# Last tile's expert rows on GpSimd, and the first token copy between two groups of control words, in a two-layer diffusion trunk with routed experts

## The reference, cut to what matters

```python
x = post_norm(x, concat([ya, yb, yc]) @ w_out[l], g_a, ln_g[l, 0], ln_b[l, 0])
h = x * (1.0 + sc_f) + sh_f
x = post_norm(x, moe_ffn(h, ...), g_f, ln_g[l, 1], ln_b[l, 1])

# moe_ffn: top-1 of 4 groups, then top-2 of the 8 experts of that group
grp = argmax(softmax(x @ w_rg)); le = (x @ w_re) of that group
top_l, top_i = top_k(le, 2); top_w = softmax(top_l) * g_w
# the tokens are sorted by expert, each expert is a gated MLP:
out = (silu(xb @ w_g[e]) * (xb @ w_u[e])) @ w_d[e]
```

## Time and profile before

| | |
|---|---|
| median of 3 runs | 1551.4 us (1550.9 to 1553.43) |
| profiled execution, its own time | 1556.95 us |
| span of its instructions | 1555.1 us |
| mean granted clock of TensorE | 0.964 of full speed |
| PE busy | 1425.6 us (92%) |
| PEld busy | 1092.0 us (70%) |
| DVE busy | 612.9 us (39%) |
| ACT busy | 335.2 us (22%) |
| POOL busy | 366.3 us (24%) |
| HBM | 341.25 MB read, 32.07 MB written |

### The profile page before, as it was taken

How to read it: one execution, slowest core, us unless ns; L and a number is a source line. 1 busy time by engine, 2 the same in 40 slices (tenths; PEclk the granted TensorE clock), 3 DMA queues, 4 the chain that set the end, 5 groups by cost and what they waited for, 6 DMA issues and landing times.

```text
span 1555.1 us, 25254 instructions
## 1 busy us (share of the span) xinstructions
PE 1425.6 (92%) x9681; PEld 1092.0 (70%) x9681; DVE 612.9 (39%) x1453; ACT 335.2 (22%) x853; POOL 366.3 (24%) x471
## 2 busy tenths in 40 slices
PE   7999999898998999997899999999888989999964
PEld 5889899665887766563488889876577876556441
DVE  1121333578378322211452123348756852221116
ACT  2211211464111111110141121236430111111102
POOL 0100015542451312111010000754227321121101
PEclk9999999999998999998999999989899989999987
DMA  9410111674817999999642111157343499999974
GB/s 381 125 65 33 64 65 36 220 284 187 327 66 280 367 387 419 419 418 418 251 125 77 47 65 33 68 169 273 141 158 127 154 363 386 420 418 418 417 293 174
DMA packets 76741, 355.37 MB, mean 229 GB/s; under 512 B 20464, under 2 KB 23792, under 8 KB 43088
## 3 DMA queue, kind: packets, MB, share of 16 engines
q1 hardware_dynamic: 43056, 292.66, 47.8%
q0 software_dynamic: 20416, 46.73, 8.3%
q10 hardware_dynamic: 13152, 14.37, 2.9%
HBM read 341.25 MB, written 32.07 MB: 240 GB/s over the span
## 4 chain that ended last, share of the span: by engine, by line
PE 75%; DVE 8%; DMA 8%; issue 4%; POOL 3%; ACT 1%; SPq 1%; ACTq 0%; DVEq 0%; POOLq 0%
PE bank L1166 22%; PE bank L1531 15%; PE bank L1552 7%; DMA ring<-in_w_exp 4%; PE bank L1402 4%; PE bank L955 2%; PE bank L1150 2%; PE bank L858 2%; PE bank L1325 2%; DMA att<-mod_rows 2%; PE bank L1512 2%; PE bank L1299 1%; PE bank L1112 1%; PE bank L1115 1%; PE bank L881 1%
## 5 line engine op out<-in xcount | busy, mean ns | idle before, releaser
L1166 PE MATMUL bank<-ring,hT 128*128 128x256 f32 (+1 forms) x1600 | 340.9, 373 | 1.1 <-DVE z L2242 1.1
L1166 PEld LDWEIGHTS bank<-ring,hT 128*128 128x128 f32 x1600 | 293.5, 192 | 37.5 <-issue 1.6
L1531 PE MATMUL bank<-z,att 128*64 128x256 f32 (+2 forms) x960 | 181.0, 398 | 10.9 <-DMA ring<-in_w_exp 10.5
L1531 PEld LDWEIGHTS bank<-z,att 128*64 128x64 f32 (+2 forms) x960 | 118.8, 152 | 49.4 <-DMA ring<-in_w_exp 11.4
L1402 PE MATMUL bank<-ring,hT 128*128 128x256 f32 x640 | 142.7, 382 | 1.7 <-ACT hT L1838 1.1
L1402 PEld LDWEIGHTS bank<-ring,hT 128*128 128x128 f32 x640 | 121.2, 192 | 17.5 <-issue 2.0
L2693 DVE TENSOR_TENSOR att<-att,bank 128x256 f32<-128x256 f32 x36 | 15.2, 421 | 272.6 <-ACT att L1927 272.6
L3028 POOL DMA_INDIRECT expert_rows<-att,cur x36 | 37.1, 1030 | 357.4 <-DVE att L2706 348.2
L1531 PE MATMUL bank<-ring,att 128*64 128x256 f32 (+2 forms) x672 | 116.9, 413 | 3.7 <-issue 3.7
L1531 PEld LDWEIGHTS bank<-ring,att 128*64 128x64 f32 (+2 forms) x672 | 71.1, 146 | 21.4 <-issue 4.2
L2242 DVE COPY z<-bank 128x512 f32<-128x512 f32 (+3 forms) x35 | 20.1, 578 | 152.5 <-PE bank L1166 152.5
(11 more groups left out here) (407 smaller groups left out, 2372.8 us busy)
## 6 DMA issues: line engine op xcount, KB each, us to landing
z<-in_w_exp SPq DMA_DIRECT2D x74, 1024.0 KB, 22.2
ring<-in_w_exp SPq DMA_DIRECT2D x72, 1024.0 KB, 19.2
ring<-in_w_ada SPq DMA_DIRECT2D x41, 1024.0 KB, 6.1
ring<-in_w_in SPq DMA_DIRECT2D x24, 1024.0 KB, 5.0
hT<-in_w_exp SPq DMA_DIRECT2D x24, 1024.0 KB, 22.9
att<-in_w_exp SPq DMA_DIRECT2D x12, 1024.0 KB, 19.4
ring<-in_w_out SPq DMA_DIRECT2D x8, 1024.0 KB, 9.9
z<-expert_rows ACTq DMA_DIRECT2D x16, 512.0 KB, 8.6
```

Of the source, the lines that this page charges most:

```text
L1166: last = eng.matmul(bk[:, i * UN:i * UN + nw], hTv[:, k, t * P:(t + 1) * P], w[:, k, 0:nw], start=(k == 0), stop=(k == KD - 1))
L1531: last = eng.matmul(bank[2 + j][c * m_:(c + 1) * m_, u * DE:(u + 1) * DE], rows, wv[c][k // 4][:, k % 4, :], start=(k == 0), stop=(k == KD ...
```

## The change

Four edits, the same in both layers. (1) The last tile's product and sum leave VectorE. `store_rows` on GpSimd now does both for tile 4: it waits for the normalised tile and for the store of tile 2, multiplies, adds and stores. (2) VectorE waits for the last rows (`h2`) before it writes `hot["pass"]`, which lies over the scale row that GpSimd reads. (3) SyncE waits for the last tile's assignment besides the last rows before the twelfth weight piece. (4) The late control words are split into `overflow_units` (lines 2666, 2668) and `overflow_turns` (lines 2670 to 2677), and VectorE's copy of the first pass's tokens, `evac_x(0)`, stands between them.

```diff
@@ sync
                 eng.wait_ge(*ev.at("h2", l, NT - 3))
                 eng.wait_ge(*ev.at("h2", l, NT - 1))
+                eng.wait_ge(*ev.at("assign", l, 1))
                 next_fixed(1)
@@ vector
                 choose_last()
-                expert_rows(NT - 1)
                 bk = jobs.bank("RK", l)
...
                 eng.tensor_scalar(kr[0:NE, 1, :], kr[0:NE, 0, :], kr[0:NE, 4, 0:1], None, ALU.is_lt).then_inc(*dve.event("outrank", l))
-                rows_shifted(NT - 1)
                 bk = jobs.bank("RR", l)
...
                 eng.tensor_tensor(turn, at, within, ALU.subtract).then_inc(*dve.step())
                 eng.wait_ge(*dve.last())
+                eng.wait_ge(*ev.at("h2", l, NT - 1))
                 eng.tensor_tensor(hot["pass"], bc(turn, 2, NLIST), bc(K["iopass"][:, 1:NLIST + 1], 1, 2 * NT),
                                   ALU.is_equal).then_inc(*dve.step())
...
                 ln_gain(1, NT - 1, m["ln"], l)
-                o1, inc = hot["past"], hot["inc"]
-                eng.tensor_tensor(o1, bc(inc[0:1, :], 1, MAXOVF), bc(K["iovf"][0:1, :], 2, NE), ALU.is_le).then_inc(*dve.step())
...
+                def overflow_units():
+                    o1, inc = hot["past"], hot["inc"]
+                    eng.tensor_tensor(o1, bc(inc[0:1, :], 1, MAXOVF), bc(K["iovf"][0:1, :], 2, NE), ALU.is_le).then_inc(*dve.step())
+                    eng.wait_ge(*dve.last())
+                    eng.tensor_reduce(ctlf[:, C_OVF:C_OVF + MAXOVF], o1, AX, ALU.add).then_inc(*dve.step())
+                    eng.wait_ge(*dve.last())
+
+                def overflow_turns():
+                    inc = hot["inc"]
+                    eng.tensor_scalar(ctlf[:, C_OVF:C_OVF + MAXOVF], ctlf[:, C_OVF:C_OVF + MAXOVF], float(NE - 1), None, ALU.min)
...
+                    eng.tensor_copy(ctl[:, C_OVF:NCTL], ctlf[:, C_OVF:NCTL]).then_inc(*dve.event("ctl", l, "late"))
...
+                overflow_units()
                 evac_x(0)
+                overflow_turns()
                 n = passes(eng, l, one_pass, turn)
@@ gpsimd
                 def store_rows(t):
                     hs = lr["hs"][:, t % 2, :]
-                    if t < NT - 2:
+                    if t == NT - 1:
+                        eng.wait_ge(*ev.at("lnhat", 1, l, t))
+                        eng.wait_ge(*ev.at("st_h2", l, t - 2))
+                        eng.tensor_tensor(hs, x[:, t, :], lr["scsh"][:, 0, 1, :], ALU.mult).then_inc(*pool.event("hsc", l, t))
+                    if t != NT - 2:
                         eng.wait_ge(*ev.at("hsc", l, t))
                         eng.tensor_tensor(hs, hs, lr["scsh"][:, 1, min(t, 1), :], ALU.add).then_inc(*pool.event("h2", l, t))
                     eng.wait_ge(*ev.at("h2", l, t))
```

More of the change, by code:

```diff
@@ L2664, in _ @@
                 ln_gain(1, NT - 1, m["ln"], l)
-                o1, inc = hot["past"], hot["inc"]
-                eng.tensor_tensor(o1, bc(inc[0:1, :], 1, MAXOVF), bc(K["iovf"][0:1, :], 2, NE), ALU.is_le).then_inc(*dve.step())
[L2667 to L2677, removed]
+                def overflow_units():
[7 more added lines that the diff above has]
+                    eng.tensor_scalar(ctlf[:, C_OVF:C_OVF + MAXOVF], ctlf[:, C_OVF:C_OVF + MAXOVF], float(NE - 1), None, ALU.min)
+                    turns_ = ctlf[:, C_TURNS:C_TURNS + 1]
+                    eng.memset(ctlf[:, C_ZERO:C_ZERO + 1], 0.0)
+                    eng.tensor_scalar(turns_, inc[0:1, NE - 1:NE], QUAD / 2 - 0.5 - OVF0, ROUND_QUAD, ALU.add, ALU.add).then_inc(*dve.step())
+                    eng.wait_ge(*dve.last())
+                    eng.tensor_scalar(turns_, turns_, QUAD - ROUND_QUAD, 1.0 / QUAD, ALU.add, ALU.mult).then_inc(*dve.step())
+                    eng.wait_ge(*dve.last())
+                    eng.tensor_copy(ctl[:, C_OVF:NCTL], ctlf[:, C_OVF:NCTL]).then_inc(*dve.event("ctl", l, "late"))
                 W = MOE[l]
```

## The result

The changed kernel is slower than the kernel before: 1557.51 us median (1554.13 to 1562.13, 22 runs) against 1553.32 (1548.08 to 1558.16, 22 runs) beside it, a ratio of 1.0028 with a 95% interval of 1.0019 to 1.0037. That is +4.3 us, between 3.0 and 5.7. The profiled execution took 1558.16 us, its span 1556.3. The forecast was +2.4 us, just inside what a measurement can tell; the change costs more, and the difference is clear of noise.

The account below looks back on a forecast made before the run. TensorE bounds the kernel (75% of the span); the routing between its long stages counts. Layer 0 +2.26 - 1.24 = +1.02, layer 1 +2.26 - 0.84 = +1.42, together +2.4 on 1551.4: 1553.8 us, range 1548.6 to 1557.0.

Parts of the forecast that it names:

- the term for TensorE: Ranks and order matmuls in the routing, counted at the high clock (0.63 and 0.22 us), no added cost.
- Part 1: Two VectorE instructions leave the routing chain, so lines 2568 and 2579 start earlier: gain 1.29 us per layer.
- Part 2: GpSimd's product and sum hold VectorE's selection of the last tile's experts: delay 3.55 us, net +2.26 per layer.
- By elements it is nearest to the second, and I let it run: Four-element tensor_scalar at line 2496 is not held by GpSimd; if held, +0.4 us in all.
- rival C: Idle TensorE runs ranks and order at the low clock: about +1.0 us per layer, 1555.8 us; chance 0.12.
- Part 3: VectorE's first token copy starts with ScalarE's, ahead of the second control words: 1.24 us earlier in layer 0, 0.84 in layer 1.
- Part 4: New waits and queue order around the last rows, weight pieces and first gather: no cost.
- the filler remains the last release: TensorE's filler at line 881 still ends after the first gather's release: SP piece goes out 1.2 us before filler's end.
- One to one: Any shift of the experts' first matmul reaches the end of the experts' stage in full.
- the 1.9 us that the prediction set as the limit of an earlier start: DMA slack in 546 to 550 us, where the weight queue waits for slots; earlier starts count in full below it.
- rival D: The moved work ends up hidden, for instance because the weights' stream sets the stage's end: unchanged, 1551.4 us; chance 0.05.
- Rivals A and B: A: no hold on these instructions, 1546.7 us, chance 0.13; B: only one GpSimd operation on the path, 1549.1 us, chance 0.10.

Follow-up runs that it names:

- warm_ranks: The changed kernel with 24 filler calls instead of 8 ahead of the last ranks; 1556.35 us, ratio 1.0024 against the kernel before.
- split_only: The kernel before with only the late control words split around the first token copy, last tile's rows still on VectorE; 1553.68 us, ratio 1.0002.
- split_again: The same kernel as split_only, timed a second time; ratio 0.9995 against the kernel before.
- filler_12_alone: The kernel before with 12 filler calls instead of 16 ahead of the first transposes, control words in one piece; 1556.16 us, ratio 1.0011.

## Why the prediction fell short

**The hold was foreseen; TensorE's clock stood in the sum at nothing.** The forecast was +2.4 us and the change cost +4.3. The time, 1557.51, lies above the stated range, whose top was 1557.0 (by its own terms, 1551.4 + 5.7, it is 1557.1). Of the 3.7 us between the forecast time of 1553.8 and the measured one, 1.9 are the base and not the change: 1551.4 was the median of three runs, and 22 runs of the same kernel have 1553.32. The step that failed is the term for TensorE: the sum let the ranks and the order run at the high clock, at no cost, although the prediction itself named their low clock as a sign of being wrong. By its own steps:

- Part 1, the gain of 1.29 us: VectorE now starts 0.04 us after TensorE's end at line 2568, as said. The gain is there, and the hold costs more than it.
- Part 2, the hold. Line 2492 ends 1.68 us later after the normalisation than 2491 did (predicted 1.79), and 2499 3.64 later than 2498 (predicted 3.55). But the step "By elements it is nearest to the second, and I let it run" was false: line 2497, four elements, was held for 2.19 us and runs after the sum. The rule set against it, the Trainium skill's "SBUF — State Buffer", section "Who interferes with whom", was right: a tensor_scalar between SBUF tiles is kept out by a running GpSimd instruction, here even by one that only writes. The operations took 2.34 us instead of 2.36 and started a little earlier, which offset it in the sum; that 3.64 came out so near 3.55 is in part luck.
- TensorE: the forecast ran the ranks at the high clock and left the low one to rival C. It came true: 1.06 against 0.63 us, with 4.66 us of idle time before them. With the order's matmul (0.28 for 0.22) that is 0.49 us per layer, the largest part of the 1.3 us by which the traces exceed the forecast. With the hold the lists came 2.68 and 2.75 us later, not 2.26. `warm_ranks` shows the part of the clock: 0.5 to 0.8 us of it. C's further part, the list matmuls at the low clock, did not come: they took 2.39 us in both layers (2.70 and 2.39 before).
- Part 3: the copy's lag behind ScalarE's fell from 1.23 to 0.07 and from 0.84 to 0.06, 1.16 and 0.78 gained against 1.24 and 0.84 predicted.
- Part 4: "the filler remains the last release" held, but that it shifts with the lists and nothing more did not. From the lists to the transposes it took 7.54 us before and 7.19 after in layer 0, and 7.93 and 8.46 in layer 1. That is -0.35 and +0.53 us that the sum had no term for, by where in the filler the clock returned. No run ties it to the change: `split_only` has 7.79 and 8.32 us there, `split_again`, the same kernel, 7.20 and 7.19.
- One to one: the gate and up matmuls of the 17th and last pass end at a fixed distance from the experts' first matmul, 202.42 us before and 202.51 after in layer 0, 202.43 and 202.43 in layer 1. Their second half, in layer 0 and layer 1, before and then after:

```profile
713.82 3.62 PE L1531 MATMUL bank<-z,att 128*64 128x256 f32 x32
1467.36 3.62 PE L1531 MATMUL bank<-z,att 128*64 128x256 f32 x32
```

```profile
716.39 3.62 PE L1532 MATMUL bank<-z,att 128*64 128x256 f32 x32
1466.03 3.62 PE L1532 MATMUL bank<-z,att 128*64 128x256 f32 x32
```

All thirteen kernels have 202.4 to 202.5 in both layers, except `filler_12_alone` with 203.9 and 204.1, longer by what its first 32 matmuls lost. The starts lie from 2.6 us earlier to 2.7 later than before, so the 1.9 us that the prediction set as the limit of an earlier start was not one. The step holds, rival D falls, and the late control words, ready at 518.70 instead of the 517.2 forecast, cost nothing. Behind these passes, in the overflow turns, the stage scatters by up to 3 us between kernels.

Layer by layer: predicted +1.02 and +1.42, found +1.20 and +2.54. Rivals A and B are excluded by the lengths of lines 2492 and 2497. Of the 4.3 us measured, 3.7 are found in the traces; the rest lies inside the interval and stays open. The result ended nearest to rival C's +4.4, for half of C's reasons, so that nearness is luck too.

## What to carry to other kernels

Work moved from VectorE to GpSimd does not run beside VectorE's work if VectorE's instructions are of the kinds held here (two tensors in SBUF, or a tensor_scalar from SBUF to SBUF with several elements per partition): each waits for the end of the running GpSimd instruction, however small it is itself. On a chain of 0.2 us instructions, count what is left of the GpSimd instruction for the first of them that falls in it, and the next GpSimd instruction for the next one. If GpSimd must be there, cut its instructions up: four pieces brought the delay of the lists from 2.7 to 0.75 and 1.00 us. And where such a hold leaves TensorE idle, price its next matmuls at both clock levels: after 4.66 us of idle time they ran at the low one in both layers, after 2.70 in one of two.

## What the runs showed of the hardware that I had not expected

A GpSimd memset (0.95 us for 128x1024 f32, against 2.34 for an operation that reads two tensors) does not hold a two-source VectorE instruction but does hold a tensor_scalar of four elements per partition. The same 32 filler matmuls took anything from 4.9 to 6.5 us at about the same place, by where the return to the high clock fell; that alone moves the experts' start by up to 1.6 us in a layer. And less filler was slower (1.0011, 1.0000 to 1.0022) with a gap of 2 us behind it, and faster (0.9983, 0.9972 to 0.9995) without.
